# First input product with both input parts as one moving operand, in 256-column groups

## The chip, the core and the metric

The kernel runs on one core of a Trainium2 chip. The metric is the device time of one execution in microseconds (us). The core has TensorE (PE in the rows; its weight loads are PEld), VectorE (DVE), ScalarE (ACT), GpSimd (POOL, not used here) and SyncE (SP), which here issues the weight transfers.

## The reference, cut to what matters

Two blocks follow one another on 256 tokens of width 2048, all in float32. The change lies in the first input product of the first block:

```python
h = rmsnorm(x, mix_pre_gain)
proj = einsum('bsd,de->bse', h, w_in)             # 256 x 2048 by 2048 x 5376
q_a, k_a, v_a, q_r, f_r, i_r, g_r = split(proj)   # 1024, 128, 128, 1024 x 4
attn = rmsnorm(sliding_window_attention(q_a, k_a, v_a, sinks))   # 16 heads, 2 of keys
rnn = hgrn2_chunkwise(q_r, f_r, i_r, g_r, lb, gain)              # f = lb+(1-lb)*sigmoid(f_r)
#     silu(q_r), values i_r, cumulative sums of log f, products in chunks, norm, * silu(g_r)
x = x + rmsnorm(concat(attn, rnn) @ w_out)
x = x + rmsnorm(relu(rmsnorm(x) @ w_up)**2 @ w_down)
```

The second block (latent attention and convolution, two layers) comes after it and is not touched.

## The kernel before

**Products.** Every float32 operand of a large product is split into a high part, which TensorE takes as float32r, and a low rest: HTh and HTl for the input (one tile HT with both, 16 tiles of 128 rows by 256 tokens), WH and WL for the weights. A product is high by high, high by low and low by high. `products` with `cols` issues three matmuls for each 128x128 weight tile (L545, L546, L547): WH by HTh, WH by HTl, WL by HTh, all with 256 moving columns into one half of a bank. `products` with `rows` (the values) makes the input the weights and streams 512 weight columns (L476 to L478). `joint_products`, used by the up projection, issues two matmuls a tile (L581, L583): WH by both parts of HT side by side (512 moving columns, a whole bank) and WL by HTh (256 columns into the bank's first half). The bank then holds the sum in its first half and the WH by HTl part in its second; the two are added afterwards.

**Halves.** Weights come in chunks of 1 MB by DMA into RAW0 to RAW3. A chunk is cut into halves of 1024 columns. ScalarE copies half j into WH (L1807, the hi part, which waits until TensorE has finished half j-4), VectorE subtracts to get WL (L1020, the low part), TensorE takes half j when WL is there. I number the halves of the first input product from 0. The keys and first values are halves 0 to 7.

**Strands.** Softmax attention, recurrence and the head outputs are generators. On every engine `Course.beat` advances each of them by one step per half: TensorE behind the matmuls of half j; ScalarE and VectorE behind the split of half j+3 and ahead of that of half j+4. Every engine has one queue in order. Banks PS0 to PS3 hold the main products in two pairs, PS4 to PS7 are handed out in turn by `small`, and a matmul that takes one waits until its last user is through.
Attention has two halves of 25 steps (scores in steps 0 to 7, maxima at 8 and 9, Exp at 10 to 13, probabilities scaled on VectorE at 12 and 14, turned on TensorE at 14 to 21 (L652) and copied by ScalarE a step later (signal `pt`), value products at 17 to 23). The recurrence has two halves of 20 steps: step 1 Ln and KK, step 2 the scan, step 3 the gaps, step 4 the LK0 operands on VectorE (`r_edge`) and the diagonal products on TensorE (QR by KK), step 5 the diagonal taken over by COPY_PREDICATED (`r_att`) and the product of LK0, from step 6 on seven levels of LQ by LK.

**Order.** Groups run as keys, queries 0, forget 0, receive 0, queries 1, forget 1, receive 1, values 0 and 1, output 0 and 1 (`MIX_ORDER`), each of 8 halves. Attention starts behind queries 0, the recurrence behind receive 0, its second half behind receive 1. ScalarE empties a group's two banks at its end with the function it needs (`store_T`: Sigmoid, Silu or copy times 0.125).

Of the kernel before, what the change touches and what calls it, by code (L numbers as in the profile page):

```python
# [23 lines left out]
MIX_ORDER = (2, 0, 3, 5, 1, 4, 6, 7, 8, 9, 10)  # L24
# [69 lines left out]
def weight_groups():  # L94

    return {
        "w_in": (16, [512, 512, 256] + [512] * 8),
# [8 lines left out]
    }  # L106

# [103 lines left out]
def weight_course(t):  # L211
# [10 lines left out]
    def weights(tensor, which, k0=0, k1=None, pair=None):  # L222
        nonlocal turn
        kts, widths = sizes[tensor]
        for g in which:
# [3 lines left out]
            for k in range(k0, k1 or kts, 8 if tensor == "w_up" else 4):  # L229
                nk = 8 if tensor == "w_up" else min(4, kts - k)  # L230
                a = kts * 128 * sum(widths[:g]) + k * 128 * w
                chunks.append(("w", t[tensor][a:a + 128 * nk * w].rearrange("(p w) -> p w", p=128), nk, w))
# [44 lines left out]
    for tensor, g, k0, k1, kts, w, pair in order:  # L277
        count = (k1 - k0) // (4 if tensor == "w_up" else 2)
        mark = None
        if k1 == kts:  # L280
# [13 lines left out]
            elif tensor == "w_up":  # L294
                mark = ("up_sum", 2 * g + 2)
            else:
                stored += 1
                mark = ("stored", stored)
# [13 lines left out]
    "va_mm va score score_in top top_neg soft_exp soft_sink soft_add probs pt_mm pt pv oa att_sq att_part att_ss att_ms att_root att_out "  # L312
# [131 lines left out]
def tensor_program(e, m, signals, plan):  # L444
# [177 lines left out]
    def attention():  # L622
        QA, KA, VA, S = m["QA"], m["KA"], m["VA"], m["S"]
        PT = Y[:, 0, 0:1536].rearrange("p (a b) -> p a b", a=4)
        for g in range(2):
            while ("query", g) not in flags:
                yield
            for n in range(25):
                if n < 8 and n % 2 == 0:
# [3 lines left out]
                    pe.wait_ge(*group["w_in", 2].taken)  # L633
                    pe.wait_ge(*group["w_in", g].taken)
# [46 lines left out]
    def recurrence():  # L681
        KK = m["KK"]
        for hh in range(2):
            while ("proj", hh) not in flags:
                yield
            qr = flat(m["QR"][:, 4 * hh:4 * hh + 4, :])
            for n in range(20):
                if n == 4:
                    for half in range(2):
                        b = small()  # L690
                        pe.wait_ge("r_key", hh + 1)
                        pe.wait_ge(*group["w_in", 5 + hh].taken)
# [25 lines left out]
    def head_outputs():  # L718
        HS, SR = m["HS"], m["S"][:, :, 0:256]
        VR = Y[:, 1, :].rearrange("p (t d) -> p t d", t=2)  # L720
        for hh in range(2):
            AD = flat(m["FR"][:, 4 * hh:4 * hh + 4, :]).rearrange("p (g t) -> p g t", g=8)
            for n in range(7):
                for i in range(2 * n, 2 * n + 2) if n < 2 else ():
# [5 lines left out]
                    pe.wait_ge(*group["w_in", 7 + hh].taken)  # L730
# [199 lines left out]
    flags.add(("proj", 1))  # L930
    for g in range(7, 9):
# [3 lines left out]
    for g in range(2):  # L935
        products(group["w_in", 9 + g], *hidden, h, cols=4)
        flags.add(("late", g))
# [66 lines left out]
def vector_program(e, m, signals, plan):  # L1004
# [76 lines left out]
    def attention():  # L1081
# [6 lines left out]
        for g in range(2):  # L1088
# [3 lines left out]
            for n in range(25):  # L1092
# [9 lines left out]
                if n < 8 and n % 2 == 0:  # L1102
# [61 lines left out]
    def recurrence():  # L1164
# [26 lines left out]
        for hh in range(2):  # L1191
            while ("proj", hh) not in flags:
                yield
            fr = flat(m["FR"][:, 4 * hh:4 * hh + 4, :])
# [77 lines left out]
    def head_outputs():  # L1272
# [22 lines left out]
        for hh in range(2):  # L1295
# [4 lines left out]
            dve.wait_ge(*group["w_in", 9 + hh].taken)  # L1300
# [314 lines left out]
    course.group(group["w_in", 2])  # L1615
    forget_bounds()
    course.group(group["w_in", 0])
    side_a = course.start(attention())
    flags.add(("query", 0))
    course.group(group["w_in", 3])  # L1620
    course.group(group["w_in", 5])
    side_r = course.start(recurrence())
    flags.add(("proj", 0))
    course.group(group["w_in", 1])
    flags.add(("query", 1))
    course.group(group["w_in", 4])
    course.group(group["w_in", 6])
    flags.add(("proj", 1))
    for g in range(7, 9):
        course.group(group["w_in", g])  # L1630
    side_h = course.start(head_outputs())
    side_m = course.start(attention_half())
    for g in range(2):
        course.group(group["w_in", 9 + g])
        flags.add(("late", g))
# [159 lines left out]
def scalar_program(e, m, signals, plan, t):  # L1795
# [61 lines left out]
    def attention():  # L1857
        S, MX, SM, OA = m["S"], m["MX"], m["SM"], m["QA"]
        PT = Y[:, 0, 0:1536].rearrange("p (a b) -> p a b", a=4)
        for g in range(2):  # L1860
            while ("query", g) not in flags:
                yield
            for n in range(25):
                if n < 8 and n % 2 == 0:
# [49 lines left out]
    def recurrence():  # L1914
# [5 lines left out]
        for hh in range(2):  # L1920
            while ("proj", hh) not in flags:
                yield
            fr = flat(m["FR"][:, 4 * hh:4 * hh + 4, :])
# [336 lines left out]
    n = group["w_in", 2]  # L2260
# [5 lines left out]
    def queries(g):  # L2266
        course.group(group["w_in", g])
        store_T(group["w_in", g], QA[:, 4 * g:4 * g + 4, :], scale=0.125)
        flags.add(("query", g))

    def forget(g):
        LB = m["LB"]
        act.wait_ge("lb_sig", 2)
        act.wait_ge(*group["w_in", 3 + g].taken)
        for i in range(4 * g, 4 * g + 4):
# [373 lines left out]
```

## Time and profile before

| | us |
|---|---|
| median of 3 runs | 1981.17 (1981.06 to 1982.47) |
| the profiled execution | 1981.26 |
| its span | 1979.4 |
| PE busy | 1954.5 (99%) |
| PEld busy | 1735.3 (88%) |
| DVE busy | 1510.5 (76%) |
| ACT busy | 1062.1 (54%) |

The granted TensorE clock is 1.00 in every stretch of the first 600 us. 95% of the chain that ended last is on PE. The first input product runs from 14.5 to 324.3 us of the span. In that stretch there is side work of the strands on all three engines.

A busy PE is not PE at its peak, since matmuls overlap: what a matmul costs is the distance of the starts, not its duration. In the rows below a start and a duration stand first, then engine, line, operation, tiles and count; in brackets the idle time ahead of it and who ended it. Rows that overlap are merged (x16) by the view.

### The profile page before, as it was taken

Reading aid. Unit: us, or ns where it says so; the run is one execution under the profiler, and the core shown is the slowest. Engines: PE = TensorE matmul, PEld = TensorE weight load, DVE = VectorE, ACT = ScalarE, POOL = GpSimd, SP = SyncE. Lnnn points to the kernel's source line nnn. Section 1 sums busy time; section 2 is a strip of 40 time slices with the busy share of each in tenths; the row PEclk is TensorE's granted clock in tenths of the full one; section 3 lists DMA queues with packets and bytes.
Section 4 is the critical chain, followed back from the end, with each engine's and each line's share of the span. In section 5 each row is a group of like instructions: output and inputs, shape, how many; then the busy total and the mean of one; then the engine's idle time right before and its main releaser. Section 6 shows DMA issues by size and latency. Waiting matters only on the chain.

```text
span 1979.4 us, 29602 instructions
## 1 busy us (share of the span) xinstructions
PE 1954.5 (99%) x12442; PEld 1735.3 (88%) x12442; DVE 1510.5 (76%) x2040; ACT 1062.1 (54%) x1507; POOL 0.2 (0%) x4
## 2 busy tenths in 40 slices
PE   7999999999999999999999999999999999999999
PEld 7999898888888888888888899999988899999887
DVE  5577775868887777788877467999866669999664
ACT  5566655465654333555544474554664656445742
POOL 0000000000000000000000000000000000000000
PEclk9999999999999999999999999999999999999999
DMA  7443445947888888889888634543455444444453
GB/s 281 150 150 128 149 149 185 359 142 297 333 339 330 333 335 332 326 326 337 337 339 342 217 125 155 189 171 132 146 192 191 149 171 174 151 165 142 160 192 125
DMA packets 63989, 442.71 MB, mean 224 GB/s; under 512 B 7248, under 2 KB 7536, under 8 KB 12400
## 3 DMA queue, kind: packets, MB, share of 16 engines
q1 hardware_dynamic: 61920, 434.30, 59.9%
q10 hardware_dynamic: 1936, 6.51, 0.9%
q8 instruction: 98, 1.61, 0.3%
q14 instruction: 35, 0.29, 0.0%
HBM read 438.67 MB, written 2.11 MB: 223 GB/s over the span
## 4 chain that ended last, share of the span: by engine, by line
PE 95%; DVE 4%; ACT 1%; DMA 0%; issue 0%; ACTq 0%; DVEq 0%
PE PS L545 13%; PE PS L546 12%; PE PS L547 12%; PE PS L476 11%; PE PS L478 11%; PE PS L477 11%; PE PS L581 11%; PE PS L468 6%; PE PS L583 6%; DVE WL L1020 1%; DVE Y L1062 0%; DMA X<-in_x 0%; PE PS L608 0%; PE PS L862 0%; DVE RAW L1029 0%; PE PS L652 0%
## 5 line engine op out<-in xcount | busy, mean ns | idle before, releaser
L1807 ACT ACTIVATE WH<-RAW 128x1024 fp32r<-128x1024 f32 (+1 forms) x636 | 663.6, 1049 | 781.0 <-PE PS L547 330.1
L1020 DVE TENSOR_TENSOR WL<-RAW,WH 128x1024 fp32r<-128x1024 f32 (+1 forms) x636 | 767.4, 1210 | 405.8 <-ACT WH L1807 404.7
L545 PE MATMUL PS<-HT,WH 128*128 128x256 f32 x1904 | 549.7, 289 | 2.4 <-DVE HT L1016 1.1
L546 PE MATMUL PS<-HT,WH 128*128 128x256 f32 x1904 | 538.8, 283 | 0.0
L547 PE MATMUL PS<-HT,WL 128*128 128x256 f32 x1904 | 538.8, 283 | 0.0
L545 PEld LDWEIGHTS PS<-HT,WH 128*128 128x128 f32 x1904 | 364.9, 192 | 18.0 <-issue 13.3
L546 PEld LDWEIGHTS PS<-HT,WH 128*128 128x128 f32 x1904 | 365.3, 192 | 0.5
L547 PEld LDWEIGHTS PS<-HT,WL 128*128 128x128 f32 x1904 | 365.0, 192 | 0.0
L581 PE MATMUL PS<-HT,WH 128*128 128x512 f32 x1024 | 357.9, 394 | 0.6 <-DVE HT L1071 0.5
L583 PE MATMUL PS<-HT,WL 128*128 128x256 f32 x1024 | 287.0, 280 | 0.0
L581 PEld LDWEIGHTS PS<-HT,WH 128*128 128x128 f32 x1024 | 191.8, 187 | 44.9 <-issue 0.7
L1029 DVE SCALAR_TENSOR_TENSOR RAW<-RAW,CB 128x2048 f32<-128x2048 f32 x96 | 219.4, 2285 | 0.0
L478 PE MATMUL PS<-WH,Ul 128*128 128x512 f32 x512 | 203.0, 397 | 0.0
L476 PE MATMUL PS<-WH,Uh 128*128 128x512 f32 x512 | 202.5, 395 | 0.0
L477 PE MATMUL PS<-WL,Uh 128*128 128x512 f32 x512 | 201.2, 393 | 0.0
L1377 DVE SCALAR_TENSOR_TENSOR UG<-UV,PK,UG 128x256 f32<-128x256 f32 x480 | 200.9, 481 | 0.2
L583 PEld LDWEIGHTS PS<-HT,WL 128*128 128x128 f32 x1024 | 193.5, 189 | 0.0
L477 PEld LDWEIGHTS PS<-WL,Uh 128*128 128x128 f32 x512 | 96.1, 188 | 24.1
L478 PEld LDWEIGHTS PS<-WH,Ul 128*128 128x128 f32 x512 | 96.1, 188 | 23.4
L476 PEld LDWEIGHTS PS<-WH,Uh 128*128 128x128 f32 x512 | 96.1, 188 | 22.5
L476 PE MATMUL PS<-WH,HT 128*128 128x512 f32 x256 | 101.3, 396 | 0.0
L478 PE MATMUL PS<-WH,HT 128*128 128x512 f32 x256 | 99.8, 390 | 0.0
(297 smaller groups left out, 1999.8 us busy)
## 6 DMA issues: line engine op xcount, KB each, us to landing
RAW<-in_w_in SPq DMA_DIRECT2D x112, 1024.0 KB, 4.7
RAW<-in_ada_w SPq DMA_DIRECT2D x96, 1024.0 KB, 5.7
RAW<-in_w_up SPq DMA_DIRECT2D x64, 1024.0 KB, 5.5
RAW<-in_w_down SPq DMA_DIRECT2D x64, 1024.0 KB, 5.1
RAW<-in_w_out SPq DMA_DIRECT2D x48, 1024.0 KB, 4.8
RAW<-in_w_pw SPq DMA_DIRECT2D x8, 1024.0 KB, 4.8
RAW<-in_w_in SPq DMA_DIRECT2D x8, 768.0 KB, 4.2
RAW<-in_w_q_up SPq DMA_DIRECT2D x6, 1024.0 KB, 4.8
```

Of the source, the lines that this page charges most:

```text
L476: e.matmul(out, sh, mh, start=st, stop=False, skip_group_check=True)
L477: e.matmul(out, sh, ml, start=False, stop=False, skip_group_check=True)
L478: return e.matmul(out, sl, mh, start=False, stop=final, skip_group_check=True)
L545: e.matmul(out, sh, ah, start=first and i % 2 == 0, stop=False, skip_group_check=True)
L546: e.matmul(out, sh, al, start=False, stop=False, skip_group_check=True)
L547: op = e.matmul(out, sl, ah, start=False, stop=final, skip_group_check=True)
L581: e.matmul(bk[i][:, 0:512], wh[:, at], m["HT"][:, kt, :, :].rearrange("p a t -> p (a t)"), start=kt == 0, stop=False, skip_group_check=True)
L583: op = e.matmul(bk[i][:, 0:256], wl[:, at], HTh[:, kt, :], start=False, stop=kt == n.kts - 1, skip_group_check=True)
L1020: e.tensor_tensor(m[f"WL{j % NHL}"][:, 0:nk * w], m[f"RAW{i % NRAW}"][:, k0 * w:(k0 + nk) * w], m[f"WH{j % NHL}"][:, 0:nk * w].bitcast(F32 ...
L1029: e.scalar_tensor_tensor(raw[:, :], raw[:, :], 1.0, m["CB"][:, :], ALU.mult, ALU.mult, accum_out=mod[:, k:k + 1]).then_inc(signals["ada"], 1)
L1377: e.scalar_tensor_tensor(UG[:, c, :], UV[:, c, j:j + 256], dw[:, c, j:j + 1], UG[:, c, :], ALU.mult, ALU.add).then_inc(signals[name], 1)
L1807: e.activation(m[f"WH{j % NHL}"][:, 0:nk * w], m[f"RAW{i % NRAW}"][:, k0 * w:(k0 + nk) * w], ACT.Copy).then_inc(signals["high"], 1)
```

## The change

The weights of `w_in` for queries, forget, receive and output are laid out in 16 groups of 256 columns (JOINT), each read in two chunks of 8 weight tiles by 256 columns; keys and values stay as they were (256 and 512 columns, chunks of 4 tiles). The 16 groups go through `joint_products`. The order of the columns stays (`KEYS`, then pairs of the former groups). ScalarE empties a group by copying the second half of both banks into the destination tile (`mix_low`); VectorE adds the first half of the banks to it in the next group, ahead of its second half (`added`, `mix_sum`); Sigmoid or Silu then runs in place over 1024 columns, once for two head pairs, in the next group ahead of its third half's side step (`finished`). The factor 0.125 moves from the queries to the keys. Attention waits two steps more in each of its halves, the recurrence one.

```diff
@@ -21,7 +21,11 @@
-MIX_ORDER = (2, 0, 3, 5, 1, 4, 6, 7, 8, 9, 10)
+KEYS, VALUES = 4, (13, 14)
+QUERIES, FORGET, RECEIVE, OUTPUT = ((0, 1), (2, 3)), ((5, 6), (7, 8)), ((9, 10), (11, 12)), ((15, 16), (17, 18))
+MIX_ORDER = (KEYS, *QUERIES[0], *FORGET[0], *RECEIVE[0], *QUERIES[1], *FORGET[1], *RECEIVE[1], *VALUES, *OUTPUT[0],
+             *OUTPUT[1])
+JOINT = tuple(g for g in MIX_ORDER if g != KEYS and g not in VALUES)
...
-        "w_in": (16, [512, 512, 256] + [512] * 8),
+        "w_in": (16, [256] * 13 + [512] * 2 + [256] * 4),
...
+    return 8 if tensor == "w_up" or tensor == "w_in" and g in JOINT else 4
...
@@ TensorE @@
-            for n in range(25):
-                if n < 8 and n % 2 == 0:
+            for n in range(-2, 25):
+                if 0 <= n < 8 and n % 2 == 0:
...
         for hh in range(2):
             while ("proj", hh) not in flags:
                 yield
+            yield
...
-    products(group["w_in", 2], *hidden, h, cols=2)
-    products(group["w_in", 0], *hidden, h, cols=4)
+    products(group["w_in", KEYS], *hidden, h, cols=2)
+
+    def joint(*groups):
+        for g in groups:
+            joint_products(group["w_in", g], h, False)
+
+    joint(*QUERIES[0])
     side_a = course.start(attention())
     flags.add(("query", 0))
-    products(group["w_in", 3], *hidden, h, cols=4)
-    products(group["w_in", 5], *hidden, h, cols=4)
+    joint(*FORGET[0], *RECEIVE[0])
     side_r = course.start(recurrence())
     flags.add(("proj", 0))
-    products(group["w_in", 1], *hidden, h, cols=4)
+    joint(*QUERIES[1])
     flags.add(("query", 1))
-    products(group["w_in", 4], *hidden, h, cols=4)
-    products(group["w_in", 6], *hidden, h, cols=4)
+    joint(*FORGET[1], *RECEIVE[1])
     flags.add(("proj", 1))
...
@@ VectorE @@
+    def added(g):
+
+        n, part = group["w_in", g], mix_tile(m, g)
+        for i in range(2):
+            dve.wait_ge("mix_low", 2 * JOINT.index(g) + i + 1)
+            tt("mix_sum", part[:, i, :], bank[2 * n.pair + i][:, 0:256], part[:, i, :], ALU.add)
...
+            for j, _ in course.begin(n):
+                if before is not None and j == n.first + 1:
+                    added(before)
...
@@ ScalarE @@
-    e.activation(KA[:, :], bank[2 * n.pair][:, 0:256], ACT.Copy)
+    e.activation(KA[:, :], bank[2 * n.pair][:, 0:256], ACT.Copy, scale=0.125)
...
+                act.wait_ge("mix_sum", 2 * JOINT.index(g) + 2)
+                part = tile[:, 4 * hh:4 * hh + 4, :]
+                e.activation(part, part, func).then_inc(signals[name], 1)
+                if kind == "f":
+                    course.start(forget(hh))
...
+            for j, _ in course.begin(n):
+                if before is not None and j == n.first + 2:
+                    finished(before)
+            before = g
+            if g in JOINT:
+                if g in OUTPUT[0]:
+                    act.wait_ge("pv", 8)
+                act.wait_ge("half_done", n.done)
+                for i in range(2):
+                    e.activation(mix_tile(m, g)[:, i, :], bank[2 * n.pair + i][:, 256:512], ACT.Copy).then_inc(
+                        signals["mix_low"], 1)
```

The side steps move against each other. ScalarE, from the last Exp pairs of the second attention half to the Ln of the recurrence's second half; S is the scores, QR the receive gate's input, E0 the Ln's output. Before, the Silu of QR stands behind all Exp, with copies of turned probabilities (Y) between it and the Ln:

```order
L1870 ACTIVATE S,SM<-S,MX 128x128
L1870 ACTIVATE S,SM<-S,MX 128x256
L1807 ACTIVATE WH2<-RAW1 128x1024 [waits half_done,raw1]
L1807 ACTIVATE WH3<-RAW1 128x1024 [waits half_done]
L2190 ACT_TABLE_LOAD
L2190 ACTIVATE QR<-PS0 128x512
L2190 ACTIVATE QR<-PS1 128x512
L1886 ACTIVATE Y<-PS4 128x384 [waits pt_mm]
L1807 ACTIVATE WH0<-RAW2 128x1024 [waits half_done,raw2]
L1886 ACTIVATE Y<-PS5 128x384 [waits pt_mm]
L1928 ACT_TABLE_LOAD [waits r_pair]
L1928 ACTIVATE E0<-FR 128x1024 [waits r_f]
```

Now, with L1915 for L1870, L2338 for L2190 and L1974 for L1928:

```order
L1915 ACTIVATE S,SM<-S,MX 128x128
L1915 ACTIVATE S,SM<-S,MX 128x256
L1852 ACTIVATE WH1<-RAW2 128x1024 [waits half_done]
L2338 ACT_TABLE_LOAD
L2338 ACTIVATE QR<-QR 128x1024 [waits mix_sum]
L1915 ACT_TABLE_LOAD
L1915 ACTIVATE S,SM<-S,MX 128x128
L1915 ACTIVATE S,SM<-S,MX 128x256
L1915 ACTIVATE S,SM<-S,MX 128x128
L1915 ACTIVATE S,SM<-S,MX 128x256
L1974 ACT_TABLE_LOAD [waits r_pair]
L1974 ACTIVATE E0<-FR 128x1024 [waits r_f]
```

The Silu moved in between two pairs of Exp, and the Ln directly behind the last pair.

TensorE, at steps 4 and 5 of the second half of the recurrence, with the main matmuls between them left out. Before (CN,S turns probabilities, Y,VA is the value product):

```order
L468 MATMUL PS7<-Y,VA 64x256 [waits pt]
L468 MATMUL PS7<-Y,VA 64x256
L468 MATMUL PS7<-Y,VA 64x128 x2
L468 MATMUL PS4<-QR,KK 128x128 [waits stored,r_key,oa]
L468 MATMUL PS4<-QR,KK 128x128 x3
L468 MATMUL PS5<-QR,KK 128x128 [waits pt]
L468 MATMUL PS5<-QR,KK 128x128 x3
...
L652 MATMUL PS6<-CN,S 128x128 [waits pt]
L652 MATMUL PS6<-CN,S 128x128 x2
L468 MATMUL PS7<-LK0 128x128 [waits r_edge,oa]
L468 MATMUL PS7<-LK0 128x128 x3
```

Now (L674 for L652, L490 for L468, LK0 named in full):

```order
L490 MATMUL PS7<-QR,KK 128x128 [waits mix_q,r_key,r_att]
L490 MATMUL PS7<-QR,KK 128x128 x3
L490 MATMUL PS4<-QR,KK 128x128 [waits pt]
L490 MATMUL PS4<-QR,KK 128x128 x3
...
L674 MATMUL PS5<-CN,S 128x128 [waits pt]
L674 MATMUL PS5<-CN,S 128x128 x2
L490 MATMUL PS6<-Y,VA 64x256 [waits pt]
L490 MATMUL PS6<-Y,VA 64x256
L490 MATMUL PS6<-Y,VA 64x128 x2
L490 MATMUL PS7<-LK0 128x128 [waits r_edge,r_att]
L490 MATMUL PS7<-LK0 128x128 x3
```

The value product moved from step 4's side to step 5's, the diagonal products take PS7 and PS4, and the LK0 product takes PS7 again and waits for `r_att` where it waited for `oa`.

## Rows read from the trace of the kernel before

**Rows 1.** Waits of TensorE, 14 to 350 us: total us, times, longest.
```profile
PE PS L468 <- DVE FR L2550: 0.7, 1, 0.7
```
**Rows 2.** Timeline of ScalarE in `products`: start, duration, engine, line, operation.
```profile
34.44 1.06 ACT L1807 ACTIVATE WH<-RAW 128x1024 fp32r<-128x1024 f32 x1 [1.33 <-PE PS L547]
...
54.54 1.06 ACT L1807 ACTIVATE WH<-RAW 128x1024 fp32r<-128x1024 f32 x1 [1.76 <-PE PS L547]
```
**Rows 3.** Timeline of ScalarE in `joint_products` of the up projection.
```profile
801.02 1.06 ACT L1807 ACTIVATE WH<-RAW 128x1024 fp32r<-128x1024 f32 x1 [1.65 <-PE PS L583]
...
807.53 0.64 ACT L2374 ACTIVATE VT<-PS 128x256 f32<-128x256 f32 x2
...
834.30 1.06 ACT L1807 ACTIVATE WH<-RAW 128x1024 fp32r<-128x1024 f32 x1 [1.65 <-PE PS L583]
```
**Rows 4.** Timeline of VectorE in the up projection: the pair of sums.
```profile
801.05 0.75 DVE L1016 TENSOR_TENSOR VT<-PS,VT 128x256 f32<-128x256 f32 x2
```
**Rows 5.** Timeline of ScalarE, 189 to 208 us: Exp, Silu, Ln.
```profile
189.89 0.39 ACT L1870 ACTIVATE S<-S,MX 128x128 f32<-128x128 f32 x1
...
191.75 1.04 ACT L1807 ACTIVATE WH<-RAW 128x1024 fp32r<-128x1024 f32 x1
...
199.86 1.06 ACT L1807 ACTIVATE WH<-RAW 128x1024 fp32r<-128x1024 f32 x1 [1.66 <-PE PS L547]
200.94 1.28 ACT L2190 ACT_TABLE_LOAD   x1
202.23 1.09 ACT L2190 ACTIVATE QR<-PS 128x512 f32<-128x512 f32 x2
...
206.34 1.06 ACT L1928 ACTIVATE E<-FR 128x1024 f32<-128x1024 f32 x1
207.30 1.04 ACT L1807 ACTIVATE WH<-RAW 128x1024 fp32r<-128x1024 f32 x1
```
**Rows 6.** Timeline of VectorE, 183 to 221 us: maxima to diagonal.
```profile
183.95 2.28 DVE L1110 TENSOR_REDUCE MX<-S 128x8 f32<-128x2048 f32 x1
...
199.37 0.16 DVE L1016 TENSOR_TENSOR SM<-SM,MX 128x8 f32<-128x8 f32 x1
...
201.69 1.22 DVE L1020 TENSOR_TENSOR WL<-RAW,WH 128x1024 fp32r<-128x1024 f32 x1
...
209.52 2.28 DVE L1208 TENSOR_TENSOR_SCAN B<-RES,E 128x1024 f32<-128x1024 f32 x1
211.72 1.20 DVE L1020 TENSOR_TENSOR WL<-RAW,WH 128x1024 fp32r<-128x1024 f32 x1
...
215.12 1.16 DVE L1020 TENSOR_TENSOR WL<-RAW,WH 128x1024 fp32r<-128x1024 f32 x1
...
218.06 1.22 DVE L1020 TENSOR_TENSOR WL<-RAW,WH 128x1024 fp32r<-128x1024 f32 x1
219.20 1.57 DVE L1237 COPY_PREDICATED FR<-CN,PS 128x512 f32<-128x512 uint32 x2
```
**Rows 7.** Timeline of TensorE, 216 to 223 us: side work and a half.
```profile
216.04 0.49 PE L652 MATMUL PS<-CN,S 128*128 128x128 f32 x3
...
217.26 2.05 PE L468 MATMUL PS<-QR,KK 128*128 128x128 f32 x16
219.07 0.48 PE L476 MATMUL PS<-WH,HT 128*128 128x512 f32 x1
219.39 0.39 PE L477 MATMUL PS<-WL,HT 128*128 128x512 f32 x1
...
221.91 0.49 PE L652 MATMUL PS<-CN,S 128*128 128x128 f32 x3
222.24 1.06 PE L468 MATMUL PS<-LK 128*128 128x128 f32 x8
```
**Rows 8.** LK0 in the first half of the recurrence, from both engines' timelines.
```profile
122.84 0.76 DVE L1016 TENSOR_TENSOR LK<-LK,FC 128x256 f32<-128x256 f32 x2
...
129.32 1.16 PE L468 MATMUL PS<-LK 128*128 128x128 f32 x8
```

More of the change, by code:

```diff
@@ L934, in tensor_program @@
     side_m = course.start(attention_half())
-    for g in range(2):
-        products(group["w_in", 9 + g], *hidden, h, cols=4)
-        flags.add(("late", g))
+    joint(*OUTPUT[0], OUTPUT[1][0])
+    flags.add(("late", 0))
+    joint(OUTPUT[1][1])
+    flags.add(("late", 1))
     course.drain(side_a, side_r, side_h, side_m)
@@ L1862, in attention @@
                 yield
-            for n in range(25):
-                if n < 8 and n % 2 == 0:
+            for n in range(-2, 25):
+                if 0 <= n < 8 and n % 2 == 0:
                     course.small_bank()
@@ L2296, in scalar_program @@
-    queries(0)
+        for kind, groups, tile, func, name in (("f", FORGET, FR, ACT.Sigmoid, "mix_f"), ("q", RECEIVE, QR, ACT.Silu, "mix_q"),
+                                               ("g", OUTPUT, GR, ACT.Silu, "mix_g")):
+            for hh in range(2):
+                if g != groups[hh][1]:
+                    continue
+                if kind == "f" and hh == 0:
+                    act.wait_ge("lb", 1)
+                    e.activation(LB[:, 0, :], LB[:, 1, :], ACT.Sigmoid).then_inc(signals["lb_sig"], 1)
+                    act.wait_ge("lb_sig", 1)
+                    e.activation(LB[:, 1, :], LB[:, 0, :], ACT.Identity, scale=-1.0, bias=ST[:, 62:63]).then_inc(
+                        signals["lb_sig"], 1)
+                act.wait_ge("mix_sum", 2 * JOINT.index(g) + 2)
[3 more added lines that the diff above has]
+                    course.start(forget(hh))
@@ new lines, in joint @@
+    def joint(before, *groups):
+        for g in groups:
+            n = group["w_in", g]
+            for j, _ in course.begin(n):
+                if before is not None and j == n.first + 2:
+                    finished(before)
+            before = g
+            if g in JOINT:
[5 more added lines that the diff above has]
+                        signals["mix_low"], 1)
@@ L2297, in scalar_program @@
+    joint(None, *QUERIES[0])
     side_a = course.start(attention())
-    projections(0)
+    flags.add(("query", 0))
+    joint(QUERIES[0][1], *FORGET[0], *RECEIVE[0])
     side_r = course.start(recurrence())
-    queries(1)
-    projections(1)
-    for g in range(2):
-        course.group(group["w_in", 7 + g])
-        store_R(group["w_in", 7 + g], lambda i: VR[:, i, 512 * g:512 * g + 512])
+    flags.add(("proj", 0))
+    joint(RECEIVE[0][1], *QUERIES[1])
+    flags.add(("query", 1))
+    joint(QUERIES[1][1], *FORGET[1], *RECEIVE[1])
@@ L2305, in scalar_program @@
+    flags.add(("proj", 1))
+    for g, n in enumerate(VALUES):
+        joint(None if g else RECEIVE[1][1], n)
+        store_R(group["w_in", n], lambda i: VR[:, i, 512 * g:512 * g + 512])
     side_h = course.start(head_outputs())
     side_m = course.start(attention_half())
-    for g in range(2):
-        course.group(group["w_in", 9 + g])
-        act.wait_ge("pv", 8)
-        store_T(group["w_in", 9 + g], GR[:, 4 * g:4 * g + 4, :], ACT.Silu)
-        flags.add(("late", g))
+    joint(None, *OUTPUT[0], OUTPUT[1][0])
@@ L2312, in scalar_program @@
+    flags.add(("late", 0))
+    joint(*OUTPUT[1])
+    finished(OUTPUT[1][1])
+    flags.add(("late", 1))
     course.drain(side_a, side_r, side_h, side_m)
-    act.wait_ge("half_done", group["w_in", 10].done)
+    act.wait_ge("half_done", group["w_in", OUTPUT[1][1]].done)
     for i in (0, 4):
@@ L2551, in predicated, with packed @@
                              data[:, :].rearrange("p (g b i) -> p g b i", b=n, i=m))
-def packed(w, widths, order=None, most=4):
+def packed(w, widths, order=None, tensor=None):
     k = w.shape[0] // 128
-    step = min(most, k)
     out, c = [], 0
-    for n in widths:
+    for g, n in enumerate(widths):
+        step = min(chunk_tiles(tensor, g), k)
         cols = w[:, c:c + n] if order is None else w[:, order[c:c + n]]
```

93 lines of the change are left out of this document (46 added, 47 removed).

## The prediction, made before the changed kernel ran

> **What bounds the kernel now.** I read the waits of TensorE first. In the stage of the first input product only one is charged to it behind the start of the keys: 0.7 us near the end of the recurrence [rows 1]. So the end is set by how long TensorE needs for its own instructions, and everything on VectorE and ScalarE is hidden as long as it comes in time. The price of a half (one pair WH, WL of 1024 columns) is read from the starts of the hi copies on ScalarE, which wait for TensorE to finish a half: seven halves of `products` from 34.44 to 54.54 us, four of 2.82 and three of 2.94 in turn, so 2.88 us in the mean of a pair [rows 2]; twelve halves of `joint_products` in the up projection from 801.02 to 834.30, so 2.773 us each [rows 3]. Both are 8 steps of one 128x128 tile: 0.360 and 0.347 us a step.
>
> The other thing to see is how late the two other engines may be. Side work n of a strand is done once per half on every engine. VectorE and ScalarE do it behind the split that TensorE's end of an earlier half released, TensorE does it at the end of its own half; a result that side step n makes on VectorE is wanted by TensorE one step later, about two halves after the release. Being late by less costs nothing, by more costs TensorE one for one.
>
> **What it removes.** Eight 512-column groups (queries, forget, receive, output, two each) become sixteen of 256. They have 64 halves in both kernels. Three matmuls of 256 columns become one of 512 and one of 256. Saved: 64 x (2.880 - 2.773) = 6.8 us. The keys and the two value groups (8 and 16 halves) stay as they are.
> The Trainium skill, page "TensorE: Matmul & The Clock Gate", section "Back-to-back issue gap", gives N/2.4 + 2.5 ns for an isolated matmul at full clock: three of 256 are then 327.5 ns and the pair 325.0, an estimate of 1.3 us for the 512 steps in place of 6.8. The two pitches of the trace, 0.360 and 0.347 us, are further apart, and I go by them.
>
> **What it adds beside TensorE.** For each of 16 groups ScalarE copies two low halves (0.64 us the pair [rows 3]) and VectorE adds them (0.75 us the pair [rows 4]): 10 us and 12 us. ScalarE loses its eight stores of 1.09 us (8.7 us) and gets six functions over 1024 columns in SBUF; the nearest row is the Ln with 1.06 us [rows 5]: 6.4 us. All of it stands beside TensorE work, and where both engines have idle time it is free. The DMA bytes, chunk sizes (1 MB), and splits per half are the same; a 1 MB chunk still serves two halves. Each group waits for the sum of the group two before; that sum is done about one and a half halves into the next group, with two and a half left, so I cost this wait at nothing.
>
> **What it moves, and what is late next.** Attention starts two side steps later in both its halves, so its second half is four steps later than before; the recurrence is one step later in its first half and (the first half being done in time) one in its second. Before, step 15 of the second attention half met step 0 of the recurrence; now step 12 does. The softmax of the first, which filled ScalarE without a pause for four side steps, now runs into the recurrence's Silu, Ln and scan. In the first half the shift is 16 to 15 only.
> I work the second half out from the end of half 54, the third half of the last receive group, as time 0.
> VectorE: the maxima of step 9 take 2.28 us and some 0.4 for the small ones behind them (the row at 183.95 [rows 6]), behind the low part of half 57; -2.77, the end of half 53, + 1.1 hi part + 1.2 low part + about 0.5 lateness from the added sum and step 8 + 2.7: 3.0.
> ScalarE, without a pause from 3.1: two heads of Exp 1.76 (189.89 to 191.75 is 1.86 with the 0.1 extra of the small Exp [rows 5]); hi part 0.95; low copies 0.64; Exp 1.86; hi 0.95; Exp 1.76; hi 1.07; table load 1.28 and Silu 1.06 on QR; table load 1.28 and the last Exp 1.8; table load 1.28 and Ln 0.97; then the hi part of half 62 starts at 19.8. (Load prices from 200.94 and 202.23, hi part 0.96 as the Ln before it, 206.34 to 207.30 [rows 5].)
> VectorE from 20.9: low part 62, 1.14; probabilities of step 14, 2.32 (199.37 to 201.69); scan 2.20 (209.52 to 211.72); low part 63 and step 3 of the recurrence, 3.40 (211.72 to 215.12); low part 64 and step 4, 2.94 (215.12 to 218.06); low part 65, 1.14; first diagonal COPY_PREDICATED, half of 1.57 [rows 6]. Sum 13.9: 34.8.
> TensorE: half 55 2.77, halves 56 to 59 at 12 x 0.228 = 2.73 each (219.39 to 221.91 is 11 matmuls in 2.52), 60 to 62 at 2.84 each behind side work (219.07 to 221.91), one turn of probabilities at 0.33 behind 59, 60 and 61 (221.91 to 222.24), the diagonal products 1.81 (217.26 to 219.07), turn and value product 1.2 behind 62 (216.04 to 217.26) [rows 7]: 26.3. There it wants PS7 for the LK0 product, and PS7 now holds the first diagonal: in the new order that matmul waits for r_att, where before it waited for oa. It stands behind two `pt` waits too (PS5 and PS6), which ScalarE clears at 28.7 and 31.6: its copies come behind a fourth table load and an Exp that needs the scan's end (26.6), a hi part each between them.
> TensorE waits 34.8 - 26.3 = **8.5 us**, in one place or in two or three close together; all further main matmuls and the low parts queue behind it. Afterwards TensorE's halves with side work take 4 to 5 us, VectorE's step some 3.1 us, so it catches up and the loss stays single. Here the skill speaks of a higher price: page "ScalarE: Activation LUTs", section "What ACT_TABLE_LOAD costs", gives a load of 1283 ns and a drain of 1380 ns at each switch; that would put 3 x 1.38 = 4.1 us more into the chain, an estimate by which the kernel would come to 1986.7 (chance 0.01, counted with rival 2). The trace has no drain there: a hi part that starts at 199.86 and takes 1.06 ends at 200.92, the load starts at 200.94 and its ACTIVATE at 202.23 [rows 5].
>
> **Small terms.** The old 0.7 us [rows 1] came of a bank that the head outputs shared with a level product of the same side step; with the recurrence a step later this pairing is gone: -0.7. Between the last output group and the second part of w_out the chain has a second sum and the Silu behind it; it grows by 0.6 to 0.8 us with some slack left. I take +0.3 of 0 to 0.8.
> First half of the recurrence: VectorE ended the LK0 preparation at 123.60 and TensorE took it at 129.32, 5.7 us later [rows 8]. Shorter halves (about 0.6), attention one step nearer (2.8) and the Silu inside a side step (about 1) leave some 1.2 us: nothing charged, but it is thin.
>
> **Sum.** Profiled execution 1981.26 (span 1979.4 and 1.9 around it; the median of the runs is 1981.17, the same): 1981.3 - 6.8 - 0.7 + 8.5 + 0.3 = **1982.6 us**. Bounds of the unknown: the waits are at least 0 (all hidden, as nearly everything was before) and at most 8.5 and the 3.0 of rival 2; I take 8.5 because each of its terms has a row.
>
> **Rivals.**
> 1. The gain comes clean: the crowding is covered, as nearly every wait before. For it: one wait of 0.7 us in some 300 us, with the same strands. Against it: the chain above, 31.7 us of work in a row on two engines against 23.2 us of TensorE. 1981.3 - 6.8 - 0.7 + 0 = 1973.8. Chance 0.20.
> 2. Slower: the first half of the recurrence collides as well. Place: the same LK0 product, half 38. If the low copies and sums (three groups, 3 x (0.64 + 0.75) = 4.2 us) stand in the chain there in place of in idle time, then it is late by 4.2 - 1.2 = 3.0 us: 1985.6. It decides from 1.2 us of lateness on. For it: the Silu and the Ln there follow each other in one side step too. Against it: the softmax has ended two side steps before them, so ScalarE starts on them nearly on time. Chance 0.15.
> 3. The saving isn't there: 768 columns are streamed for a step in either case, and if the joint step costs 0.360 us here, where the strands put side matmuls between the halves, nothing is saved: 1982.6 + 6.8 = 1989.4. Against it: both pitches [rows 2, 3] are of the same operands HT, WH and WL. Chance 0.04. By the issue-gap section of the Trainium skill's TensorE page 1.3 us would remain, an estimate of 1988.1.
>
> **How the numbers follow.** About 0.2% (4 us) is what a measurement of this kernel can tell from no change: 1977.3 to 1985.1 is same. Forecast case 0.56, its own range 1979.5 to 1985.5 (0.02 falls below same, 0.03 above); rival 1 0.20; rival 2 0.15 (0.12 slower, 0.03 same); rival 3 0.04; a wait of 2 to 5 us 0.05 (0.02 faster, 0.03 same). Faster 0.24, same 0.57, slower 0.19. The range from 1973.5 to 1987.0 takes in rival 1 and rival 2 and leaves out the highest cases.
>
> **What would show it.** Right: joint halves without side work of 2.77 us; one cluster of TensorE waits of 7 to 10 us between about 200 and 225 us, charged to VectorE's FR (COPY_PREDICATED) or LK0 and to ScalarE's copies of turned probabilities, at L490 and L674; no wait of 0.7 us at the head outputs; from w_out on everything as before, shifted. Wrong: no wait there at all (then the alignment or the priced chain is wrong), or waits at two places, around 120 and around 210 us (rival 2), or joint halves of 2.86 us (rival 3).

## The result: slower, 1989.6 us

| | median us | lowest to highest | runs |
|---|---|---|---|
| before | 1981.17 | 1981.05 to 1982.47 | 5 |
| after | 1989.57 | 1988.96 to 1991.06 | 5 |

Ratio 1.0044, 95% interval 1.0032 to 1.0055: 8.4 us slower, where 1982.6 was forecast and 1987.0 was the end of the range. The profiled execution took 1988.96 us (span 1987.2).

**Where the time went.** The second product (w_out) starts at 332.03 us; before it started at 324.29. That is +7.74 of the +7.8 us in the span, so everything lies ahead of it. First the waits of TensorE from 20 to 345 us, read as in [rows 1] (engine, what it was about to do, its releaser: total, times, longest):

```profile
PE PS L490 <- ACT Y L1931: 3.3, 3, 2.0
PE PS L674 <- ACT Y L1931: 2.6, 1, 2.6
PE PS L490 <- DVE FR L1265: 1.6, 1, 1.6
PE PS L490 <- DVE S L1127: 0.7, 1, 0.7
PE PS L490 <- DVE LK L1043: 0.3, 1, 0.3
```

The 0.7 us of before is gone; 8.5 us are new. TensorE's own timeline shows the cluster (in brackets the idle time before the instruction):

```profile
218.16 1.16 PE L490 MATMUL PS<-QR,KK 128*128 128x128 f32 x8 [0.90 <-ACT Y L1931]
...
224.71 0.90 PE L674 MATMUL PS<-CN,S 128*128 128x128 f32 x3 [2.63 <-ACT Y L1931]
227.59 1.55 PE L490 MATMUL PS<-Y,VA 128*64 128x256 f32 x8 [1.98 <-ACT Y L1931]
...
230.72 2.08 PE L490 MATMUL PS<-LK 128*128 128x128 f32 x8 [1.58 <-DVE FR L1265]
```

Four waits, 7.1 us: three for ScalarE's copies of turned probabilities, the last one for the COPY_PREDICATED on VectorE, which frees PS7. VectorE had the operands of the LK0 product ready at 228.9 us, so the bank alone can account for the last 1.6 us at most; no run gave that product another bank. Look at the durations too: the three matmuls of a turn of probabilities take 0.90 us where they took 0.49 in [rows 7]. The stretches show why (columns: window and length, then busy us with instruction counts of PE, PEld, DVE, ACT, POOL, then the granted TensorE clock as a share of 2.4 GHz, DMA share, GB/s):

```profile
214.00:224.00 10.00, 7.18 (x40) 5.71 (x39) 7.12 (x10) 6.79 (x9) 0.00 (x0) 1.00 0.07 29
224.00:234.00 10.00, 5.73 (x23) 4.27 (x24) 9.73 (x14) 5.85 (x11) 0.00 (x0) 0.51 0.62 204
234.00:244.00 10.00, 10.00 (x59) 8.23 (x58) 6.26 (x9) 5.18 (x8) 0.00 (x0) 0.97 0.33 112
```

TensorE stood at the lower of its two levels, 1.2 GHz, for some ten microseconds. Read microsecond by microsecond, the granted clock was 1.00 up to 224 us and 0.50 from 225, so it fell inside the first long wait (222.1 to 224.7 us); it rose again between 234 and 235. VectorE is the engine without a pause there, 9.73 of 10 us. Its timeline and ScalarE's, against [rows 5, 6]:

```profile
207.94 1.28 ACT L2338 ACT_TABLE_LOAD   x1
209.23 1.06 ACT L2338 ACTIVATE QR<-QR 128x1024 f32<-128x1024 f32 x1
210.31 1.28 ACT L1915 ACT_TABLE_LOAD   x1
...
213.48 1.28 ACT L1974 ACT_TABLE_LOAD   x1
214.78 1.06 ACT L1974 ACTIVATE E<-FR 128x1024 f32<-128x1024 f32 x1
215.74 1.99 ACT L1852 ACTIVATE WH<-RAW 128x1024 fp32r<-128x1024 f32 x2
```
```profile
216.81 1.22 DVE L1047 TENSOR_TENSOR WL<-RAW,WH 128x1024 fp32r<-128x1024 f32 x1 [5.63 <-ACT WH L1852]
...
220.28 2.28 DVE L1236 TENSOR_TENSOR_SCAN B<-RES,E 128x1024 f32<-128x1024 f32 x1
...
229.95 1.54 DVE L1265 COPY_PREDICATED FR<-CN,PS 128x512 f32<-128x512 uint32 x2
```

Last the price of a joint half. In TensorE's timeline eight steps (one half) from 45.48 to 48.31 us, and eight from 97.86 to 100.63:

```profile
45.48 0.40 PE L603 MATMUL PS<-HT,WH 128*128 128x512 f32 x1
...
48.31 0.40 PE L603 MATMUL PS<-HT,WH 128*128 128x512 f32 x1
...
97.86 0.39 PE L603 MATMUL PS<-HT,WH 128*128 128x512 f32 x1
...
100.63 0.39 PE L603 MATMUL PS<-HT,WH 128*128 128x512 f32 x1
```

2.83 and 2.77 us, for the same instructions. Most undisturbed halves of the first product cost the higher price: all from 31.35 to 92 us do.

### The profile page after: what moved, and what is told of

Its sections match the earlier page's. It is cut to its first block, busy times and chain, and to the rows that moved or that the text cites. A ratio compares the mean times of both kernels' runs of the same rounds, so it can differ in the third digit from the quotient of the medians.

```text
span 1987.2 us, 28644 instructions
## 1 busy us (share of the span) xinstructions
PE 1953.8 (98%) x11930; PEld 1708.7 (86%) x11930; DVE 1520.6 (77%) x2072; ACT 1069.8 (54%) x1530; POOL 0.2 (0%) x4
## 4 chain that ended last, share of the span: by engine, by line
PE 91%; DVE 5%; ACT 3%; issue 1%; DMA 1%; SPq 0%; ACTq 0%; DVEq 0%
PE PS L603 15%; PE PS L498 11%; PE PS L500 11%; PE PS L499 11%; PE PS L567 9%; PE PS L568 9%; PE PS L569 9%; PE PS L605 8%; PE PS L490 6%; DVE WL L1047 1%; ACT WH L1852 1%; ACT S L1915 1%; PE PS L630 0%; DVE Y L1089 0%; PE PS L885 0%
## 5 line engine op out<-in xcount | busy, mean ns | idle before, releaser
L603 PE MATMUL PS<-HT,WH 128*128 128x512 f32 x1536 | 542.0, 397 | 0.6 <-DVE HT L1098 0.5
L567 PE MATMUL PS<-HT,WH 128*128 128x256 f32 x1392 | 401.6, 288 | 2.8 <-DVE HT L1098 1.4
L568 PE MATMUL PS<-HT,WH 128*128 128x256 f32 x1392 | 393.8, 283 | 0.0
L603 PEld LDWEIGHTS PS<-HT,WH 128*128 128x128 f32 x1536 | 288.0, 187 | 70.2 <-issue 3.7
L567 PEld LDWEIGHTS PS<-HT,WH 128*128 128x128 f32 x1392 | 266.9, 192 | 13.8 <-issue 8.7
L568 PEld LDWEIGHTS PS<-HT,WH 128*128 128x128 f32 x1392 | 267.0, 192 | 0.4
L498 PE MATMUL PS<-WH,HT 128*128 128x512 f32 x256 | 101.5, 396 | 0.0
L499 PE MATMUL PS<-WL,HT 128*128 128x512 f32 x256 | 100.1, 391 | 0.0
```

Source lines behind the costliest of these rows:

```text
L498: e.matmul(out, sh, mh, start=st, stop=False, skip_group_check=True)
L499: e.matmul(out, sh, ml, start=False, stop=False, skip_group_check=True)
L567: e.matmul(out, sh, ah, start=first and i % 2 == 0, stop=False, skip_group_check=True)
L568: e.matmul(out, sh, al, start=False, stop=False, skip_group_check=True)
L603: e.matmul(bk[i][:, 0:512], wh[:, at], m["HT"][:, kt, :, :].rearrange("p a t -> p (a t)"), start=kt == 0, stop=False, skip_group_check=True)
```

## The experiments

In all of them the medians of before were 1981.15 to 1981.85 us, and each is compared within its own round of runs. Theory: the second attention half stands too close to the recurrence (alignment). Rival: the new copies, sums and functions are too much work there (load). The intervals of e2, e7 and e8 include 1: these can't be told from the kernel before.

| run | us | ratio to before, 95% interval |
|---|---|---|
| e1 attention two earlier | 1978.37 | 0.9986 (0.9976 to 0.9996) |
| e2 recurrence two later | 1980.56 | 0.9998 (0.9988 to 1.0007) |
| e3 before, with the shifts | 1989.76 | 1.0044 (1.0029 to 1.0059) |
| e4 the waits filled | 1987.98 | 1.0033 (1.0020 to 1.0046) |
| e5 e1, first recurrence later | 1977.90 | 0.9981 (0.9972 to 0.9989) |
| e6 e1, attention not delayed | 1985.57 | 1.0019 (1.0010 to 1.0028) |
| e7 e1, low part first | 1980.59 | 0.9996 (0.9987 to 1.0005) |
| e8 e1, three matmuls | 1981.20 | 1.0000 (0.9990 to 1.0009) |
| e9 e1, 512, 512, 256, 256 | 1976.50 | 0.9975 (0.9965 to 0.9985) |
| e10 e5 and e9 together | 1975.32 | 0.9968 (0.9956 to 0.9981) |
| e11 recurrence at once | 1989.10 | 1.0036 (1.0022 to 1.0049) |

**e1: attention.**

```diff
-            for n in range(-2, 25):
+            for n in range(0 if g else -2, 25):
```

> The changed kernel, with the second half of attention started two side steps earlier (the recurrence stays where the change put it), on all three engines. Theory (alignment): the cluster of TensorE waits around 214 to 232 us (7.1 us, with the lower clock level behind it, about 3 us) comes from the Exp steps that run into the recurrence's Silu, Ln and scan; two steps less of overlap take 3.6 us of Exp and 2.3 us of probabilities out of the chain, so 0 to 2.6 us of wait are left there and the clock stays at 1.00: 1979.4 to 1982.0 us. Rival (load): the waits come from the new copies, sums and the Silu that ScalarE and VectorE got, wherever the strands stand: at least 5 us of wait remain, 1986 or more.

1978.37 us, 1.0 us below the theory's range and faster than before. Nothing of the cluster is left; all waits of TensorE from 20 to 345 us:

```profile
PE PS L490 <- ACT Y L1931: 0.4, 1, 0.4
PE PS L490 <- DVE LK L1043: 0.4, 1, 0.4
PE PS L490 <- DVE S L1127: 0.2, 1, 0.2
```

The granted clock is 1.00 in every stretch. The added work is the same as in the changed kernel, so load alone doesn't make the cluster.

**e2: recurrence.**

```diff
-            yield
+            for _ in range(3 if hh else 1):
+                yield
```

> The changed kernel, with the second half of the recurrence started two more side steps later (attention stays). The same two steps less of overlap from the other side. Theory (alignment): as in the run with attention earlier, the cluster goes but for 0 to 2.6 us: 1979.4 to 1982.0 us, if the recurrence, now ending two halves later, is still done before the end of the output groups (its last side matmuls stood at about half 85 of 88; if it ends too late, TensorE waits once near 325 us, up to 3 us, 1985). Rival (load): at least 5 us of wait remain, 1986 or more.

1980.56 us, inside the range: the same distance from the other side cures as well, less completely. 3.0 us of waits stay, none longer than 0.9, 1.5 of them between 215 and 235 us; the clock stays at 1.00. It matters that two strands are apart, not which one moves.

**e3: the shifts alone.** In the kernel before: `range(25)` becomes `range(-2, 25)` in both halves of attention, and the recurrence yields once more.

> The kernel before, with only the two shifts of the change (attention two side steps later in both halves, recurrence one later); products stay as three matmuls of 256 columns. Theory (alignment): the shifts alone make a cluster of 5 to 7 us of TensorE waits near 215 to 235 us and bring the clock down behind it: 1989 to 1991 us. Rival (load): without the joint groups' copies and sums the crowding is covered, at most 1 us of wait, 1981 to 1982.

1989.76 us, as slow as the changed kernel, with none of its new products:

```profile
PE PS L468 <- ACT Y L1888: 2.3, 1, 2.3
PE PS L652 <- ACT Y L1888: 1.7, 1, 1.7
PE PS L468 <- DVE FR L1239: 1.6, 1, 1.6
PE PS L652 <- DVE S L1134: 0.6, 1, 0.6
```
```profile
224.00:234.00 10.00, 5.57 (x24) 4.22 (x25) 9.73 (x14) 5.65 (x11) 0.00 (x0) 0.66 0.59 210
```

5.6 of the 6.2 us are three waits for the same releasers as in the changed kernel, ended at 224.52, 227.39 and 230.53 us; the fourth, 0.6 us at 211.59, is for probabilities on VectorE, which the changed kernel doesn't have. The clock is at 0.66 in this stretch. So the shifts alone cost 8.6 us (1989.76 against 1981.15), as much as the whole change. The added work has a share: 7.1 us in the cluster of the changed kernel against 6.2 here at most, and the 1.4 us of small waits elsewhere don't appear here.

**e4: the price of the clock.** 22 matmuls of 512 columns into a bank that is cleared later, ahead of the last three waits of the cluster:

```diff
+                    if g and n == 17:
+                        fill(10)
                     b = small()
                     pe.wait_ge("probs", ...)
...
+                    if g and n == 17:
+                        fill(7)
...
+                    if hh:
+                        fill(5)
                     b = small()
                     pe.wait_ge("r_edge", 4 * hh + 4)
```

> The changed kernel, with 22 matmuls of 512 columns whose result is thrown away put in front of the three longest waits (10, 7 and 5 of them, 2.3, 1.6 and 1.1 us at 0.228 us each), so that TensorE works in the time in which it waited; nothing else moves. Theory (clock): the granted clock stays at 1.00 through 214 to 240 us, the waits recorded fall by about 5 us, and the time falls by what the lower level cost behind them: 1986.3 to 1987.6 us. Rival: the lower clock cost nothing of its own, since the two other engines set the pace there: 1989.6, the same as the changed kernel.

1987.98 us, 1.6 us below the changed kernel; I had expected 2.0 to 3.3. TensorE has 22 matmuls more to do and is sooner done. The waits fell from 8.5 to 4.5 us, and the clock didn't fall:

```profile
224.00:234.00 10.00, 8.04 (x44) 5.67 (x43) 9.73 (x14) 6.05 (x11) 0.00 (x0) 1.00 0.59 198
```

The timeline says where the 1.6 us are (LK is the LK0 product, CN,S the next side work, a half of main matmuls between them):

```profile
230.91 1.16 PE L490 MATMUL PS<-LK 128*128 128x128 f32 x8 [0.87 <-DVE FR L1278]
...
234.67 0.49 PE L683 MATMUL PS<-CN,S 128*128 128x128 f32 x3
```

3.76 us from the one to the other; in the changed kernel from 230.72 to 236.23, 5.51 us. That is 1.75 us, the price of the lower level behind the last wait. The slow matmuls ahead of 230.7 cost nothing: VectorE let the LK0 product go at the same time in both (230.72 and 230.91), so they only ate waiting time. The Trainium skill, page "TensorE: Matmul & The Clock Gate", section "HAM oscillation — how this bites in real kernels", says that gaps in TensorE's work bring it back to half its clock. The trace agrees with that, 0.51 behind the waits and 1.00 where they were filled.

**e8: what the joint operand saves.** On e1, in the first product only:

```diff
-                    e.matmul(bk[i][:, 0:512], wh[:, at], m["HT"][:, kt, :, :].rearrange(...), start=kt == 0, ...)
+                    e.matmul(bk[i][:, 0:256], wh[:, at], HTh[:, kt, :], start=kt == 0, ...)
+                    e.matmul(bk[i][:, 256:512], wh[:, at], HTl[:, kt, :], start=False, ...)
```

> The kernel e1, with the 512-column matmul of each joint step in the first input product split again into two of 256 columns (same banks, groups, copies, sums and order; w_up stays joint). Measures what the joint operand alone saves. Theory (pitch of this stretch): 64 halves go from 2.83 (the level of 16 of 19 undisturbed halves in 31 to 101 us) to 2.88 us: +3.2 us, 1981.6 us. Rival (the level that I took for the prediction, 2.773): +6.8 us, 1985.2 us. Second rival: nothing is saved, 1978.4 us.

1981.20 against 1978.37: 2.8 us, near the theory's 3.2 and far from my 6.8. The same figure can be read where w_out starts, first e1, then e8 (timeline of TensorE):

```profile
321.03 0.39 PE L498 MATMUL PS<-WH,AH 128*128 128x512 f32 x1
```
```profile
323.82 0.40 PE L498 MATMUL PS<-WH,AH 128*128 128x512 f32 x1
```

e8 has no wait in this stage and e1 has 1.0 us, so the matmuls alone saved 3.8 us, of which 1.0 went into small waits.

**Two levels.** The trace of the kernel before had shown both, in the up projection. Its first pass (175 and 319 steps without an interruption between the first and the second row, and the third and the fourth):

```profile
430.85 0.40 PE L581 MATMUL PS<-HT,WH 128*128 128x512 f32 x1
...
491.18 0.39 PE L581 MATMUL PS<-HT,WH 128*128 128x512 f32 x1
...
492.26 0.39 PE L581 MATMUL PS<-HT,WH 128*128 128x512 f32 x1
...
604.62 0.40 PE L581 MATMUL PS<-HT,WH 128*128 128x512 f32 x1
```

60.33 us over 174 steps are 0.3467, 112.36 over 318 are 0.3533; times 8, 2.77 and 2.83. The level changed at one interruption (0.40 us between two starts that are 0.12 apart otherwise), and kept. Nor does it belong to the place: in e4 the first part of the same pass, the same instructions, ran at 2.83. First and last row of the pass, changed kernel and e4:

```profile
428.76 0.47 PE L603 MATMUL PS<-HT,WH 128*128 128x512 f32 x1 [0.52 <-DVE HT L1098]
...
612.36 0.40 PE L603 MATMUL PS<-HT,WH 128*128 128x512 f32 x1
```
```profile
427.20 0.47 PE L603 MATMUL PS<-HT,WH 128*128 128x512 f32 x1 [0.52 <-DVE HT L1111]
...
611.58 0.40 PE L603 MATMUL PS<-HT,WH 128*128 128x512 f32 x1
```

183.60 and 184.38 us, at a granted clock of 1.00 in both.

**e7: low part first.** `wl` with 256 columns ahead of `wh` with 512 from the second tile of a group on.

> The kernel e1, with the two matmuls of each joint step in the other order (256 columns of WL first, then 512 of WH) from the second tile of a group on, in the first input product and in w_up. The traces show two levels for a joint half, 2.773 and 2.827 us, each kept until the next interruption, and the same place of the code on either level in different runs. Theory (the level is set by how a stretch of joint steps is entered): another order of entry changes the level of some stretches; w_in between 1975 and 1979 us in total if they go down, up to 3.4 us more in w_up's second pass (64 halves at 2.773 now) if they go up: 1975 to 1982 us. Rival (the level belongs to the place or to the other engines' load): every stretch keeps its level, 1978.4 us.

1980.59 us. The levels moved: w_out started at 319.90 us against 321.03 in e1, and the second pass of the up projection, at 2.77 before, took 180.4 us for its 64 halves in place of 177.2, which is more than the 2.2 us that the kernel lost. In this order the alternation is broken at every border of a group (two matmuls of 512 columns follow each other there), and between two borders each undisturbed stretch has one of the two levels. Two groups of the up projection's first pass, one behind the other, without a wait between them (29 steps from the first row to the second, and from the third to the fourth):

```profile
432.53 0.40 PE L606 MATMUL PS<-HT,WH 128*128 128x512 f32 x1
...
442.59 0.62 PE L606 MATMUL PS<-HT,WH 128*128 128x512 f32 x2
443.63 0.40 PE L606 MATMUL PS<-HT,WH 128*128 128x512 f32 x1
...
453.87 0.40 PE L606 MATMUL PS<-HT,WH 128*128 128x512 f32 x1
```

10.06 us over 29 steps are 2.775 for eight, 10.24 are 2.825. Most groups of that pass have the higher level, the one from 488.78 to 498.83 the lower, and all sixteen of the second pass the higher. Averages over several groups lie between the levels; no undisturbed group does. So a level changes where the alternation is broken, which speaks against the rival of a level fixed by place or load; but the same instructions at the border led now to the one level and now to the other, so their order alone doesn't decide which.

**e9: long, long, short, short.** The loop over i is run twice, first for the 512-column matmuls, then for the 256-column ones.

> The kernel e1, with the four matmuls of one tile of a joint group in the order 512, 512, 256, 256 columns in place of 512, 256, 512, 256 (first input product and w_up). From rows: 512-column matmuls follow each other every 0.227 to 0.233 us and 256-column ones every 0.120 us, so a pair costs 0.347 to 0.353 us, the two levels that are there now. Theory (the price of a step is that of its matmuls, not of their order): the levels stay within 2.77 to 2.83 us per half, 1976 to 1981 us. Rival (the two levels come from the alternation of long and short matmuls): one level only, 2.77 (1973.0 us: 55 halves in w_in and 39 in w_up fall by 0.054) or 2.83 (1982 us).

1976.50 us, 1.9 below e1. One level everywhere, but neither 2.77 nor 2.83: six steps take 2.09 us in both stages, 2.79 per half (first product, then up projection):

```profile
45.25 0.63 PE L603 MATMUL PS<-HT,WH 128*128 128x512 f32 x2
...
47.34 0.62 PE L603 MATMUL PS<-HT,WH 128*128 128x512 f32 x2
...
799.68 0.62 PE L603 MATMUL PS<-HT,WH 128*128 128x512 f32 x2
...
801.77 0.63 PE L603 MATMUL PS<-HT,WH 128*128 128x512 f32 x2
```

The rival (the two levels come from the alternation of long and short) is right in kind and wrong in its number.

**e5: the first half of the recurrence one later.** `for _ in range(1 if hh else 2): yield`, on e1.

> The kernel e1 (second half of attention two side steps earlier), with the first half of the recurrence one side step later too. e1 took 1978.37 us and had three waits of TensorE left, 0.4 us (value product, behind a copy on ScalarE), 0.4 us (the LK0 product at 130.36 us) and 0.2 us. Theory (alignment holds for the first half as well): the LK0 wait goes, the value product's stays or goes: 1977.6 to 1978.4 us. Rival: the later first half brings a new wait further on, as the run e2 had (3.0 us in four places): 1980 or more.

1977.90 us: one wait of 0.4 us is left, the LK0 wait is gone. w_out starts 1.1 us earlier than in e1; 0.8 of it is lost again in the first pass of the up projection, which fell on the higher level (184.38 us, as in e4).

**e6: no delay in the first half of attention.** `range(25)` in both halves, on e1.

> The kernel e1, without the two side steps of delay in the first half of attention as well: the first score product is now asked for at the end of half 16 (56.8 us). In the trace of the changed kernel VectorE ended the last query sum at about 60.0 us. Theory (the delay was needed for the first scores): one wait of TensorE of about 3.2 us at 56.8 us, less the 0.8 us of the two waits in the first half, which go since the softmax is two steps further from the recurrence: 1980.5 to 1981.0 us. Rival: VectorE comes to the sum earlier or the wait is made good later: 1977.6 to 1978.4 us.

1985.57 us (1983.7 to 1987.7 in its ten runs), a miss by 4.6 to 5.1. The wait of 3.1 us came where it was expected, and behind it what I had left out again:

```profile
57.00:60.00 3.00, 0.03 (x1) 0.00 (x0) 1.79 (x3) 1.06 (x1) 0.00 (x0) 0.97 0.77 251
60.00:62.00 2.00, 1.84 (x9) 1.19 (x10) 0.18 (x2) 0.00 (x0) 0.00 (x0) 0.50 0.35 147
62.00:64.00 2.00, 2.00 (x7) 1.71 (x8) 0.48 (x1) 0.00 (x0) 0.00 (x0) 0.50 0.01 4
64.00:66.00 2.00, 2.00 (x8) 1.71 (x7) 0.00 (x0) 0.00 (x0) 0.00 (x0) 0.50 0.00 0
66.00:68.00 2.00, 2.00 (x11) 1.75 (x11) 0.00 (x0) 0.94 (x1) 0.00 (x0) 0.83 0.00 0
```

A single gap, and some 7 us at the lower level: 7 and 8 matmuls in two microseconds, where the stretch from 68 to 70 us has 15. w_out starts 7.4 us later than in e1: 4.4 of it are waits (5.4 against 1.0, two new ones of 0.9 and 0.8 among them), the other 3.0 have no wait and fit the clock. So the first half of attention needs a delay (a single step was not tried), and only the second half must not inherit it.

**e11: the second recurrence one step earlier.** `if hh == 0: yield`, in the changed kernel.

> The changed kernel, with the second half of the recurrence one side step earlier (the extra step of the change taken back there, kept in the first half). Step 11 of the second attention half meets step 0 of the recurrence (12 in the changed kernel, 14 in e1 and e2). Theory (alignment): TensorE asks for the diagonal and the LK0 product one half earlier (2.8 us), the chain behind it gets shorter by at most one Exp of 1.8 us: 1 to 2.8 us more of waiting, with up to 1 us more at the lower clock level: 1990.5 to 1993.5 us. Rival (load): unchanged, 1989.6 us.

1989.10 us, where the theory had 1990.5 to 1993.5; the number is the rival's. One wait of 6.4 us stands ahead of the LK0 product at 225.72, now for its operands on VectorE (`r_edge`) and not for PS7, with one of 1.0 before it: 7.4 us, against 7.1 in the changed kernel. TensorE asked earlier, but the chain ended 5.0 us earlier as well: with the Ln ahead of the Silu ScalarE has three table loads there in place of four, and the scan ran at 211.45 in place of 220.28. My step "the chain gets shorter by at most one Exp" was wrong. The run therefore doesn't decide against the alignment (e1, e2 and e3 are the tests of that); it says that the wait doesn't grow with every step of nearness.

**e10: both cures.** e5 and e9 in one kernel.

> The kernel e5 (second half of attention two side steps earlier, first half of the recurrence one later; 1977.90 us) with the order of matmuls of e9 (512, 512, 256, 256 columns for each tile of a joint group). Theory (the two act in different terms and add up): e9 took 1.9 us off e1 (1976.50 against 1978.37), e5 had started w_out 1.1 us earlier than e1 but lost 0.8 us of it to a higher level in w_up's first pass, which e9's order doesn't have (one level of about 2.79): 1976.5 - 1.1 = 1975.4 us, 1975.0 to 1976.0. Rival (the gain of e9 came of a lucky entry, as e5's loss came of an unlucky one): 1976.5 to 1978.5 us.

1975.32 us, as the sum said. The kernel before took 1981.85 in this round and 1981.17 beside the changed kernel, so e10 is 5.9 to 6.5 us faster than it (0.3%), and 14.3 us faster than the changed kernel (1989.57). One wait of 0.5 us is left in the stage.

## Why the prediction was wrong, point by point

The time was forecast as 1982.6; the profiled execution took 1989.0. The step that failed is the first term of the sum, the saving by the joint products: 6.8 us were put down, 3.4 to 3.8 came. Two smaller ones were put at nothing: the lower clock behind the waits (1.75 us) and small waits elsewhere (1.4 us). The large term, 8.5 us of waiting, was right. The steps in the order of the sum:

- **The joint products save 6.8 us: wrong, the mis-sized term.** The price 2.773 per half came of twelve halves of the second pass [rows 3]. The first product ran mostly at 2.83; e8 measures 2.8 us in time and 3.8 in matmuls. With 64 x 0.053 = 3.4 us for the saving, the error is +3.4. Rival 3, with a chance of 0.04, named the place where it failed; its 2.86 has no row (its own 0.360 us a step makes 2.88). The Trainium skill, page "TensorE: Matmul & The Clock Gate", section "Back-to-back issue gap", would give 1.3 us of saving, an estimate; the runs lie between it and my rows.
- **The old wait of 0.7 us goes: right.** It is in no list.
- **The second half of the recurrence waits 8.5 us: right, and nearly all of its working too.** The first item has a slip: its terms add up to 2.7, not to the 3.0 that I wrote, and ScalarE's Exp started at 199.05, which is 3.1 as I went on with; by the terms as they stand the wait would have come out at 8.2, so a part of the exactness is luck. From the end of half 54 (195.97) I had ScalarE's hi part of half 62 at 19.8, so 215.8: it started at 215.74. The scan, behind low part and probabilities, at 24.4, so 220.3: 220.28. The two `pt` waits were to clear at 28.7 and 31.6, so 224.7 and 227.6: 224.71 and 227.59. The diagonal's end at 34.8, so 230.8: the LK0 product went at 230.72. By the working TensorE wanted it at 26.3, so 222.3, which makes 8.45 us; 7.1 of them are on record as waits, the rest is mostly slow matmuls between them. (The window I named for it, 200 to 225 us, was earlier than this working; it stood from 217 to 231.) e1, e2 and e3 show that the alignment makes it. The table loads had no drain behind them: ended at 209.22, its ACTIVATE at 209.23.
- **"Afterwards ... the loss stays single": wrong.** No term stood for the clock. Behind 230.72 the lower level cost 1.75 us, and filling the waits gave 1.6 back. The trace of before has no long wait and so no row for this; a forecast of 8.5 us of waiting in one place should have left its range open for it.
- **First half, "nothing charged, but it is thin": nearly.** Waits of 0.4 (copy on ScalarE, 116.53 us) and 0.3 us (LK0, 130.31) came there, rival 2 at a quarter of its 3.0 us; with 0.7 us at 185.61 (for VectorE's L1127, a score), of which nothing was said, 1.4 us. e5 takes the LK0 wait away.
- **The end chain costs 0.3 us: no.** No wait stands there, and w_out's shift is the kernel's.

1982.6 + 3.4 + 1.75 + 1.4 - 0.3 = 1988.9, against 1989.0 measured. The sum closes better than its terms are known: with e8's 3.8 for the saving it would be 1988.5. The signs by which rival 3 was to be known (2.86 against 2.77) were drawn too coarsely for a world in which 2.83 is possible.

## What to carry to other kernels

When a strand of side work is moved, look at what then meets it two or three steps later on the other engines; the strands need their distance, and here one changed line, the same on three engines, that starts one of them earlier turned 8.4 us of loss into 2.8 of gain. A wait of a few microseconds on TensorE can cost more than itself, by what runs at the lower clock behind it (1.75 us in the changed kernel, 3.0 in e6); price both. A steady pitch is read in several stretches before it is multiplied by 512 steps.

## What the runs showed of the hardware that was not expected

- Alternating matmuls of 512 and 256 columns run at 0.3467 or 0.3533 us a pair, at a granted clock of 1.00: the one for 512 pairs in a row (up projection, second pass, changed kernel), the other for 495 (first pass, e4). An interruption of 0.4 us changed the level, as did a border between groups in e7, where nothing waited, and the same instructions had the one level in one kernel and the other in the next. In the order 512, 512, 256, 256 it was 0.348 throughout. What decides between the two stays open.
- The granted clock fell to 0.5 inside a wait of 3.1 us (e6), one of 6.4 (e11), the first of three of 2.6, 2.0 and 1.6 us (the changed kernel) and the second of three of 1.7, 2.3 and 1.6 us (e3). Waits of 0.9 us and less, 3.0 us in all (e2), and of 1.1 and less (e4) left it at 1.00.
